# A fused two-model forward pass on one core: hidden tiles turned by VectorE in 32×32 blocks, and forget gates with the narrow operand stationary

## What is computed

```
def swiglu(n, w_gate, w_up, w_down):
    return (jax.nn.silu(n @ w_gate) * (n @ w_up)) @ w_down      # 1024 -> 2816 -> 1024, five times
...
log_f = jax.nn.log_sigmoid(f_f.astype(jnp.float32) + b_forget[l].astype(jnp.float32))
c = jnp.cumsum(log_f, axis=1).transpose(0, 2, 1)                # bias of the forgetting attention
```

## Time and profile before

| | us |
|---|---|
| median of 3 runs (lowest, highest) | 1378.33 (1377.07, 1378.73) |
| the profiled execution | 1376.84 |
| its span, first to last instruction | 1375.1 |
| busy in it: PE, DVE, ACT | 1366.6, 853.6, 774.4 |
| L1223, residue with gain: 592 instructions on DVE | 413.8 |
| L2072, transposes of `hid` on PE: 210 instructions | mean 0.271 each |
| idle of PE that the view of waits puts down to another engine, largest | 1.1 |

### The profile page before, as it was taken

One profiled execution on the slowest core, in us unless ns is written; L12 is line 12 of the kernel. 1 busy time (PEld: TensorE's weight loads), 2 busy tenths in 40 slices (PEclk: granted clock), 3 DMA queues, 4 the chain that ended last, 5 costly groups with the idle time before them and its releaser, 6 DMA issues.

```text
span 1375.1 us, 19419 instructions
## 1 busy us (share of the span) xinstructions
PE 1366.6 (99%) x6466; PEld 1135.6 (83%) x6466; DVE 853.6 (62%) x1350; ACT 774.4 (56%) x1251; POOL 50.0 (4%) x86
## 2 busy tenths in 40 slices
PE   9999999999999999999999999999999999999999
PEld 7888888888888888888888888888888888888887
DVE  6655556767655557755556676555566756665553
ACT  6555556645655546655556675555566675655552
POOL 1000010000000001000001010000002000000000
PEclk9999999999999999999999999999999999999999
DMA  8766626665666654766663347666455654575560
GB/s 292 233 205 218 214 92 203 214 202 169 199 200 204 191 176 138 229 195 189 190 198 100 120 134 240 204 190 186 152 144 179 201 169 138 168 230 183 185 209 33
DMA packets 198292, 251.57 MB, mean 183 GB/s; under 512 B 17922, under 2 KB 136928, under 8 KB 198240
## 3 DMA queue, kind: packets, MB, share of 16 engines
q1 hardware_dynamic: 197968, 250.86, 57.9%
q0 software_dynamic: 224, 0.03, 0.0%
q10 hardware_dynamic: 48, 0.02, 0.0%
HBM read 249.80 MB, written 1.05 MB: 182 GB/s over the span
## 4 chain that ended last, share of the span: by engine, by line
PE 95%; DVE 2%; ACT 1%; issue 1%; DMA 0%; SPq 0%; POOL 0%; DVEq 0%; ACTq 0%
PE ps L1933 30%; PE ps L1935 30%; PE ps L1934 29%; PE ps L1959 2%; PE ps L2072 2%; DMA raw<-in_ffn_w_up 0%; PE ps L2236 0%; PE ps L2588 0%; PE ps L2416 0%; PE ps L2417 0%; ACT whi L610 0%; DVE wlo L1226 0%; PE ps L2263 0%; POOL stat L586 0%; SPq L334 0%
## 5 line engine op out<-in xcount | busy, mean ns | idle before, releaser
L1223 DVE SCALAR_TENSOR_TENSOR wlo<-raw,gcol,whi 128x512 fp32r<-128x512 f32 x592 | 413.8, 746 | 274.0 <-ACT whi L610 273.9
L1933 PE MATMUL ps<-whi,kthi 128*128 128x512 f32 (+2 forms) x1384 | 548.4, 396 | 1.4 <-DVE wlo L1223 1.1
L1935 PE MATMUL ps<-whi,ktlo 128*128 128x512 f32 (+2 forms) x1384 | 537.1, 388 | 0.0
L1934 PE MATMUL ps<-wlo,kthi 128*128 128x512 f32 (+2 forms) x1384 | 536.3, 388 | 0.0
L610 ACT ACTIVATE whi<-raw,gcol 128x512 fp32r<-128x512 f32 x592 | 392.2, 714 | 228.5 <-PE ps L1935 223.2
L1935 PEld LDWEIGHTS ps<-whi,ktlo 128*128 128x128 f32 x1384 | 259.8, 188 | 54.3
L1933 PEld LDWEIGHTS ps<-whi,kthi 128*128 128x128 f32 x1384 | 260.0, 188 | 54.0 <-issue 1.9
L1934 PEld LDWEIGHTS ps<-wlo,kthi 128*128 128x128 f32 x1384 | 260.3, 188 | 48.9
L1231 DVE TENSOR_TENSOR wlo<-raw,whi 128x1024 fp32r<-128x1024 f32 x140 | 169.9, 1223 | 108.7 <-ACT whi L614 108.3
L614 ACT CAST whi<-raw 128x1024 fp32r<-128x1024 f32 x140 | 145.5, 1050 | 129.8 <-PE ps L1935 129.8
L1933 PE MATMUL ps<-whi,hthi 128*128 128x512 f32 x400 | 156.0, 390 | 0.0
(11 more groups left out here) (243 smaller groups left out, 807.2 us busy)
## 6 DMA issues: line engine op xcount, KB each, us to landing
raw<-in_ffn_w_gate SPq DMA_DIRECT2D x176, 256.0 KB, 2.9
raw<-in_ffn_w_up SPq DMA_DIRECT2D x176, 256.0 KB, 3.1
raw<-in_ffn_w_down SPq DMA_DIRECT2D x160, 256.0 KB, 3.4
raw<-in_w_in SPq DMA_DIRECT2D x80, 256.0 KB, 3.4
raw<-in_gmlp_w_in SPq DMA_DIRECT2D x64, 256.0 KB, 3.2
raw<-in_w_gate SPq DMA_DIRECT2D x44, 256.0 KB, 2.8
raw<-in_w_up SPq DMA_DIRECT2D x44, 256.0 KB, 3.1
raw<-in_w_down SPq DMA_DIRECT2D x40, 256.0 KB, 3.3
```

The source lines that it names most:

```text
L1223: ins = nc.vector.scalar_tensor_tensor(out=wlo[:, s, cut], in0=raw[:, s, cut], scalar=gcol[:, k:k + 1], in1=f32(whi[:, s, cut]), op0=ALU.m ...
L1933: nc.tensor.matmul(dst, lhs[0], rhs[0], start=first, stop=False)
L1934: nc.tensor.matmul(dst, lhs[0], rhs[1], start=False, stop=False)
L1935: return nc.tensor.matmul(dst, lhs[1], rhs[0], start=False, stop=last)
```

## The change

Three things change.

1. For all tiles but the last of each block, the turning of `hid` goes from PE to DVE. Sixteen `STREAM_TRANSPOSE` instructions each take 32 partitions of `hid`, with four blocks of 32×32 in the free direction, and write them turned into another group of 32 partitions of `hid_turned`, which lies in `sq_out` in SBUF. ACT and DVE (`turned_hidden`) read that in place of bank 6. The 50 `hid_flip` calls (200 transposes) of PE are gone; in their place PE waits for `hid_ready` before it writes a bank that the gated tile reads. The last tile of each block is still turned by PE.
2. In `ffn_first` the 16 stand between gated half 1 and the residue of slot 3; in the loop, between the gated halves and the residue of slot 3; in ffn10 after the residue of slot 3 and ahead of the copy of the values and the residues that `keys_values(1)` needs.
3. For the forget gates the 16 or 8 weight columns are stationary and all 256 tokens stream: 16 matmuls, where there were 32. The result has heads on partitions, so ACT copies it to SBUF (`f_t`), PE turns it by two small transposes ahead of slot 2 of tile 3, and ACT reads those with the scale.

```diff
+        hid_turned = sq_out[:, 0:TT * FT]
...
@@ ACT, turned_hidden
-                    act.wait_ge(sem("hid_full"), j + (b + 1))
-                    nc.scalar.copy(hthi[:].rearrange("p c n -> p (c n)"), ps[:, 6, :]).then_inc(sem("ht_high"), 1)
+                    act.wait_ge(sem("hid_turned"), j + (turned + 1))
+                    nc.scalar.copy(hthi[:].rearrange("p c n -> p (c n)"), hid_turned).then_inc(sem("ht_high"), 1)
...
@@ ACT, MIX2 tiles 1 to 3
-                for s in range(3):
+                for s in range(2):
                     more(s)
+                if n == 3:
+                    act.wait_ge(sem("f_turned"), 1)
+                    for t in range(TT):
+                        ins = nc.scalar.activation(st("f16", 32)[:, 16 * t:16 * t + 16], ps[:, 1, 16 * t:16 * t + 16], ACT.Copy,
+                                                   scale=st(f"r_pre_mix2{t}"))
+                    ins.then_inc(sem("f_ready"), 1)
+                more(2)
...
+                if n == 2:
+                    act.wait_ge(*f_done)
+                    nc.scalar.copy(f_t, ps[0:16, 0, 0:S]).then_inc(sem("f_read"), 1)
...
@@ DVE
+            def hid_turn(n):
+
+                dve.wait_ge(sem("hid_ready"), n)
+                for i in range(4):
+                    rows = slice(32 * i, 32 * i + 32)
+                    for j in range(4):
+                        ins = nc.vector.transpose(
+                            hid_turned[32 * j:32 * j + 32, :].rearrange("p (c t i x) -> p i c t x", c=2, t=2, i=4)[:, i],
+                            hid[rows, :, :].rearrange("p t (c j x) -> p j c t x", c=2, j=4)[:, j])
+                ins.then_inc(sem("hid_turned"), 1)
+
             def ffn_first(name, pre):
...
                 gated_tile(1, pre, count("silu_done"))
+                hid_turn(seen["silu_done"])
                 more(3)
...
                     for t in range(TT):
                         gated_tile(t, pre, j * 2 + (b + t + 1))
+                    hid_turn(j * 2 + (b + 2))
                     low(3, j + base[3], name)
...
@@ DVE, hybrid layer
+            lows([0, 1], "mix2")
             dve.wait_ge(sem("f_ready"), 1)
+            mark(nc.vector.memset(cum4, 0.0))
...
             fox_squares(0, "foxq")
-            lows([0, 1, 2], "mix2")
+            lows([2], "mix2")
...
@@ PE, ffn_rest
-                def hid_flip(j):
-
-                    pe.wait_ge(sem("hid_ready"), j * 2 + (b + 2))
-                    for t in range(TT):
-                        ins = hid_turn(6, t, lambda c: c * S + t * P)
-                    ins.then_inc(sem("hid_full"), 1)
...
                 gate_up(1, 0)
                 if amid:
                     amid()
-                if flip_free:
-                    pe.wait_ge(*flip_free)
-                hid_flip(0)
+                pe.wait_ge(sem("hid_ready"), b + 2)
                 gate_up(1, 1)
...
                 down(0, first=True)
-                hid_flip(1)
                 with pe.Fori(2, NF - 1) as j:
+                    pe.wait_ge(sem("hid_ready"), j * 2 + b)
                     tile_product(lambda s: j + base[s])
                     down(j - 1)
-                    hid_flip(j)
...
@@ PE, hybrid layer
-            def forget_gates(c, t):
...
+            def forget_gates(c):
+                nc.tensor.matmul(ps[0:16, 0, 0:S], f_high_low[:, c, :], kthi[:, c, :], start=c == 0, stop=False)
+                ins = nc.tensor.matmul(ps[0:8, 0, 0:S], f_high_low[:, c, 0:8], ktlo[:, c, :], start=False, stop=c == KC - 1)
...
+            def turn_gates():
+                pe.wait_ge(sem("f_read"), 1)
+                for t in range(TT):
+                    ins = nc.tensor.transpose(ps[:, 1, 16 * t:16 * t + 16], f_t[:, t * P:(t + 1) * P], ident[0:16, 0:16])
+                ins.then_inc(sem("f_turned"), 1)
```

More of the change, by code:

```diff
@@ L653, in ffn_rest @@
                 base, b = [n - 1 for n in use], seen.get("hid_full", 0)
+                turned = seen.get("ffns", 0) * (NF - 1)
                 def turned_hidden(j):
-                    act.wait_ge(sem("hid_full"), j + (b + 1))
-                    nc.scalar.copy(hthi[:].rearrange("p c n -> p (c n)"), ps[:, 6, :]).then_inc(sem("ht_high"), 1)
+                    act.wait_ge(sem("hid_turned"), j + (turned + 1))
+                    nc.scalar.copy(hthi[:].rearrange("p c n -> p (c n)"), hid_turned).then_inc(sem("ht_high"), 1)
                 def turned_tile(t):
-                    act.wait_ge(sem("hid_full"), b + NF + t)
+                    act.wait_ge(sem("hid_full"), b + 1 + t)
                     cut = slice(t * P, (t + 1) * P)
@@ L1265, in turned_hidden @@
                     dve.wait_ge(sem("ht_high"), j + (b_ht + 1))
-                    nc.vector.tensor_tensor(htlo[:].rearrange("p c n -> p (c n)"), ps[:, 6, :],
+                    nc.vector.tensor_tensor(htlo[:].rearrange("p c n -> p (c n)"), hid_turned,
                                             f32(hthi[:]).rearrange("p c n -> p (c n)"), ALU.subtract
@@ L1979, in flip_h, with tile_product @@
                 flip(t, lambda c, t: h[:, t, c * P:(c + 1) * P], ready=renewed)
-            def tile_product(n_of, bank=4, between=None, beside=None):
+            def tile_product(n_of, bank=4, between=None, beside=None, at=3):
                 for s in range(4):
                     made(s, n_of(s))
-                    if s == 3 and between:
+                    if s == at and between:
                         between()
@@ L1991, in tile_product @@
                             ins = product(ps[:, bank + t, :], kt(k, t), rhs, k == 0, k == KC - 1)
-                            if beside:
-                                beside(k, t)
+                        if beside:
+                            beside(k)
                     ins.then_inc(slot_used[s], 1)
@@ L2147, in last_half @@
                     return ins
+                pe.wait_ge(sem("hid_ready"), b + 2 * last)
                 gate_up(last, 0).then_inc(sem("tile0_done"), 1)
@@ L2154, in ffn_rest @@
                 pe.wait_ge(sem("hid_ready"), b + 2 * last + 1)
+                if flip_free:
+                    pe.wait_ge(*flip_free)
                 hid_turn(6, 0, lambda c: c * P).then_inc(sem("hid_full"), 1)
@@ L2464, in _, with mix2_tile @@
                 take(s)
-            def mix2_tile(n, beside=None):
+            def mix2_tile(n, beside=None, between=None):
                 if n >= 2:
                     pe.wait_ge(sem("mix_read"), 2 * (n - 1))
-                tile_product(lambda s: use[s], bank=MIX2_BANK[n], beside=beside)
+                tile_product(lambda s: use[s], bank=MIX2_BANK[n], beside=beside, between=between, at=2)
                 for s in range(4):
@@ L2491, in _ @@
             made(4, take(4))
-            def forget_gates(c, t):
[L2494 to L2501, removed]
-                    if c == KC - 1 and t == TT - 1:
-                        ins.then_inc(slot_used[4], 1)
+            def forget_gates(c):
+                nc.tensor.matmul(ps[0:16, 0, 0:S], f_high_low[:, c, :], kthi[:, c, :], start=c == 0, stop=False)
+                ins = nc.tensor.matmul(ps[0:8, 0, 0:S], f_high_low[:, c, 0:8], ktlo[:, c, :], start=False, stop=c == KC - 1)
+                if c == KC - 1:
+                    ins.then_inc(slot_used[4], 1)
+            def turn_gates():
[3 more added lines that the diff above has]
+                ins.then_inc(sem("f_turned"), 1)
             mix2_tile(2, forget_gates)
-            mix2_tile(3)
+            mix2_tile(3, between=turn_gates)
             pe.wait_ge(sem("r_rotated"), 1)
```

22 lines of the change are left out of this document (8 added, 14 removed).

## The result

The changed kernel takes 1386.58 us (median of 4 runs, 1385.62 to 1386.79), the kernel before, run beside it, 1377.78 (median of 4, 1377.07 to 1378.73): a ratio of 1.0062 with a 95% interval of 1.0045 to 1.0079. Forecast were 1368.6 us and a range of 1362 to 1379. The profiled execution has a span of 1383.9 us, 8.8 more than before.

A forecast was written before the change was run, and what follows sets the result against it. TensorE, busy 99% of the span, was taken to bound the kernel. Transposes removed −23.5, forget gates −1.5 and new waits +15.3 sum to −9.7 us, from 1378.33 to 1368.6 us; range 1362 to 1379.

The forecast's parts named there:

- Transposes off PE, 23.5 us: On PE's path, 50 sets of four transposes removed at 0.47 us each: 23.5 us saved (22.0 to 24.5).
- Forget gates, 1.5 us: MIX2 tile 2 on PE: 32 small matmuls at 3.67 us become 2.16, saving 1.5 us (0.9 to 2.0).
- T = 16 × 0.22 = 3.5 us: VectorE's time for the 16 transposes of a tile, 0.22 us each: 3.5 us (2.2 to 5.4).
- the crossing of groups: On VectorE, given as a reason for transposes at 0.34 us each: they cross partition groups, which the trace doesn't show.
- the 311 ns of a bf16 tile: Skill page's VectorE transpose price; as the pace of each of the 16, T 5.0 us and the sum −2.4.
- Hidden in the loop: DVE in a loop pass: 9.59 us busy plus 3.5 stays hidden; DVE bounds the loop only from T = 6.7.
- End of a block: Last `turned_hidden` before its reader on PE, 2.7 us of room: no cost at T 3.5, perhaps 0.5 us at 5.4.
- The waits at tile 1, 4 × 3.1 + 2.9: PE waits for late residues at slot 3 in four blocks and for `keys_values(1)` in ffn10: 15.3 us together.
- After a wait TensorE goes on as before: TensorE behind the five waits: the sum −23.5 − 1.5 + 15.3 holds no term for a slower clock.
- third rival: Five pauses of 3 us slow TensorE's clock behind them, 1.7 us each, 8.4 in all: 1377.0 us; chance 0.12.
- The slow start: Program's first 14 matmuls on TensorE take 3.35 us, 0.24 each, against 0.12 later; cited for the slowed clock.
- dear transposes: VectorE transposes at 0.34 us, T 5.4, waits 24.8: 1380.6 us; decides from about 0.31 each; chance 0.13.

The follow-up runs named there:

- runs 12 and 13: TensorE turns tile 0, VectorE the other tiles: with the old forget gates 1357.04 us, with the new 1355.41 us (ratios to the kernel before 0.9851 and 0.9840).
- runs 7 and 10: Changed kernel, transposes writing the partition group they read, or the next one, groups kept for four in a row: 1372.21 and 1373.92 us.
- runs 7 to 10: Changed kernel with its 16 transposes per tile in four other orders of partition groups read and written: 1372.21, 1387.25, 1384.56 and 1373.92 us.
- run 4: Changed kernel with only the first 11 of tile 0's 16 transposes issued in each block: 1376.32 us, ratio 0.9989 to the kernel before.
- after: The changed kernel itself in its profiled execution, against the kernel before: span 1383.9 us.
- run 1: Changed kernel with tile 0's turning put behind the residue of slot 3 (third block: behind those of ukv as well): 1361.54 us, ratio 0.9886.
- run 5: Changed kernel with only the first 7 of tile 0's 16 transposes issued in each block: 1363.27 us, ratio 0.9897 to the kernel before.
- run 11: Changed kernel with tile 0 turned by TensorE and, in tiles 1 to 9, each VectorE transpose issued twice: 1511.54 us.
- run 8: Changed kernel, transposes in the other order: group written stays for four, group read changes each time: 1387.25 us, ratio 1.0077.
- run 9: Changed kernel, transposes inside their own partition group, the group changing with each instruction: 1384.56 us.
- runs 6 and 11: Changed kernel with each transpose issued as two halves, 1397.49 us; and with tile 0 by TensorE, the other tiles' transposes issued twice, 1511.54 us.

## Why the prediction was wrong

- *Transposes off PE, 23.5 us.* Right: 24.1, from 0.49 a pass.
- *Forget gates, 1.5 us.* Right: tile 2 at 12.95 (13.0 forecast), 1.2 to 1.3 net in the traces, 1.6 between the medians of runs 12 and 13.
- *T = 16 × 0.22 = 3.5 us.* **The first step that failed**: the price of one transpose. T is 5.05. The rows behind the 0.22 are pairs that follow each other in the same partitions, and for such pairs the estimate was good: 0.19 to 0.20 where the groups stay, 0.22 on average in runs 7 and 10. The 16 transposes are another case, since each changes a group. The prediction named the crossing of groups as a possible price, but crossing is free; it did not ask what each instruction changes against the one ahead of it. The section of the Trainium skill named at runs 7 to 10 would have raised the question. The prediction weighed another one (the 311 ns of a bf16 tile, by which T would have been 5.0), near the 0.317 measured, but for an instruction of another shape.
- *Hidden in the loop.* Right, with 7.2 us of room (forecast 6.7).
- *End of a block: nothing at 3.5, perhaps 0.5 at 5.4.* Right in kind: 0.27 each at 5.05.
- *The waits at tile 1, 4 × 3.1 + 2.9.* The place and the mechanism were right in all five blocks. By the prediction's own formula T = 5.05 gives 4.6 and 4.4, and PE stood still for 4.56 to 4.63. The term's size was off by the transposes' price alone: 23.0 instead of 15.3.
- *After a wait TensorE goes on as before.* **The second step that failed**, silently in the forecast and openly in its third rival. The sum has no term for it. The granted clock falls to 0.50, 1.2 GHz, behind these waits and takes 9.8 us. The prediction gave this 0.12, because no long pause stood in the trace before. The slow start was the only witness and pointed the right way; that it is the same effect isn't shown, since the granted clock reads 1.00 there too. The Trainium skill (TensorE: Matmul & The Clock Gate, Why this matters for your kernels) warns that an idle gap between bursts of matmuls puts the clock back, and here the trace agrees in all five blocks, behind waits of 4.4 to 4.5 us.

The errors add: +7.7 for the waits, +9.8 for the clock, +1.35 and +0.3 for the ends and MLA, −0.6 and +0.3 for the first two terms, −0.3 for the start, which is the 18.5 us between the forecast for the profiled execution (1367.1) and its 1385.6. Either failure alone would have given about no change: dear transposes (0.317, just past the 0.31 where that rival decides) −9.7 + 7.7 + 1.35 = −0.7 us, and the clock alone about 1376 (run 4). The chances took these rivals one at a time, 0.13 and 0.12, and had both together only as a part of the 0.12 for slower, though the dearer transpose makes the longer wait and the longer wait brings the lower clock more often; together they lie above the upper end of the range.

## What to carry to other kernels

Work taken off a full engine is worth its time only if what replaces it isn't ahead of something that this engine is about to need: the same 16 instructions cost 24.5 us more in one place than one line later, and keeping tile 0's turning on TensorE saved 5.2 more, so move or keep the one instance that stands at a tight spot. On TensorE a wait of a few microseconds has a second price, the half clock behind it. In these kernels waits up to 1.7 us never had it, those of 2.4 to 3.1 us had it in 27 of 39 cases and those of 4.4 us and more in every case, and where counted (after, runs 1, 4, 6 to 10) it was 1.4 to 3.0 us. Price a row of VectorE instructions by neighbours that change partition groups as they will.

## What the runs showed of the hardware that was not expected

- *Which waits bring the lower clock.* Waits of 1.5 to 1.7 us: in none of five blocks (run 5), nor behind the 15 of 1.0 to 1.6 us in run 11. Of 2.4 to 2.6 us: behind 16 of 23 (run 11; the lower clock begins at most 0.5 us before the wait ends and at most 1.0 us after). Of 2.8 to 3.1 us: in four of five (run 4), three of five (7), three of five (10), and in run 1 the only one. Of 4.4 us: in all 14 (after, run 8, and four in run 9, whose fifth, of 3.5 us, did not). Of 5.1 to 6.5 us: in all ten (runs 6 and 11). So from 2.4 to 3.5 us a wait of the same length in the same program does it in one place and not in another; why is open.
- *What one costs.* The nine matmuls in ffn01 lost 1.7 us, the 13 in ffn2 2.6, behind waits of the same 4.4 us; the largest loss, 3.0 us, stands in run 10 behind a wait of 2.95. Of each, 0.1 is the first step after the wait, which is that much longer without the lower clock too (run 5).
- *VectorE's neighbours.* For transposes of 32×128 float32 the next one starts 0.19 to 0.20 us later in the same groups, 0.31 to 0.32 when a group changes, whether it is read or written, and whether or not data crosses.
